# Stick-breaking attention in a hybrid block: two heads' steps taken in turn, on two halves of the PE array

## What is computed

```python
def stick_breaking_attention(q, k, v):
    """A[t,s] = sigmoid(z_ts) prod_{s<j<t} (1 - sigmoid(z_tj)), s < t; q, k, v (B, S, H, d)."""
    ...
        z = jnp.einsum('bqhd,bkhd->bhqk', qb, k).astype(jnp.float32) * scale
        mask = kpos[None, :] < qpos[:, None]
        log_1m = jnp.where(mask, jax.nn.log_sigmoid(-z), 0.0)
        rest = lax.cumsum(log_1m, axis=3, reverse=True) - log_1m
        wts = jnp.where(mask, jnp.exp(jax.nn.log_sigmoid(z) + rest), 0.0)
        return jnp.einsum('bhqk,bkhd->bqhd', wts.astype(v.dtype), v)
```

## Time and profile before

| | us |
|---|---|
| median of the three runs | 3531.89 |
| the three runs | 3523.72, 3532.70, 3531.89 |
| the profiled execution: its time | 3528.36 |
| its span | 3526.5 |

### The profile page before, as it was taken

How to read it: one execution, slowest core, us unless ns; L and a number is a source line. 1 busy time by engine, 2 the same in 40 slices (tenths; PEclk the granted TensorE clock), 3 DMA queues, 4 the chain that set the end, 5 groups by cost and what they waited for, 6 DMA issues and landing times. The chain is left out here.

```text
span 3526.5 us, 59587 instructions
## 1 busy us (share of the span) xinstructions
PE 3337.7 (95%) x24514; PEld 2835.4 (80%) x24514; DVE 2334.9 (66%) x3196; ACT 1581.9 (45%) x2553; POOL 482.5 (14%) x399
## 2 busy tenths in 40 slices
PE   8999999899999899999998999999999989889998
PEld 8998676778998699886767789986899856659986
DVE  7877476448875588754744488755887258658852
ACT  5552435236552455524352365524655253645541
POOL 0003113540003000031125300030000100310001
PEclk9999999999999999999999999999999999999999
DMA  4235211012235223452100122342333222122331
GB/s 157 100 131 186 73 60 38 3 49 96 103 132 160 72 108 108 137 162 73 65 26 4 49 96 103 135 158 73 126 108 106 86 68 72 44 82 85 108 104 64
DMA packets 81589, 327.38 MB, mean 93 GB/s; under 512 B 11904, under 2 KB 11904, under 8 KB 65832
## 3 DMA queue, kind: packets, MB, share of 16 engines
q1 hardware_dynamic: 81320, 323.57, 26.9%
HBM read 321.15 MB, written 4.74 MB: 92 GB/s over the span
## 5 line engine op out<-in xcount | busy, mean ns | idle before, releaser
L235 DVE TENSOR_TENSOR w_low<-w_raw,w_high 128x1024 fp32r<-128x1024 f32 (+1 forms) x241 | 340.2, 1412 | 466.0 <-ACT w_high L227 465.1
L227 ACT ACTIVATE w_high<-w_raw 128x1024 fp32r<-128x1024 f32 (+1 forms) x241 | 284.5, 1182 | 538.0 <-PE ffa_ps L253 172.5
L833 DVE TENSOR_TENSOR w_low<-w_raw,w_high 128x1024 fp32r<-128x1024 f32 (+1 forms) x186 | 220.9, 1187 | 21.4 <-ACT w_high L712 10.7
L712 ACT ACTIVATE w_high<-w_raw 128x1024 fp32r<-128x1024 f32 (+1 forms) x186 | 190.2, 1023 | 3.0 <-PE ffa_ps L253 1.6
L251 PE MATMUL mix_proj_ps<-mix_x_high,w_high 128*128 128x512 f32 x416 | 171.8, 413 | 12.2 <-DVE mix_x_low L400 12.0
L253 PE MATMUL mix_proj_ps<-mix_x_high,w_low 128*128 128x512 f32 x416 | 167.4, 402 | 0.0
L252 PE MATMUL mix_proj_ps<-mix_x_low,w_high 128*128 128x512 f32 x416 | 166.4, 400 | 0.0
L251 PE MATMUL ffa_ps<-ffa_hid_high,w_high 128*128 128x512 f32 x352 | 141.7, 402 | 1.7 <-DVE w_low L235 1.7
L251 PE MATMUL b_f_ps<-b_f_hid_high,w_high 128*128 128x512 f32 x352 | 139.3, 396 | 1.7 <-DVE w_low L235 1.7
L252 PE MATMUL b_f_ps<-b_f_hid_low,w_high 128*128 128x512 f32 x352 | 139.0, 395 | 0.0
L253 PE MATMUL b_f_ps<-b_f_hid_high,w_low 128*128 128x512 f32 x352 | 138.9, 395 | 0.0
(11 more groups left out here) (739 smaller groups left out, 10978.0 us busy)
## 6 DMA issues: line engine op xcount, KB each, us to landing
ffa_quarters<-in_ffa_seven SPq DMA_DIRECT2D x40, 1024.0 KB, 4.8
ffb_quarters<-in_ffb_seven SPq DMA_DIRECT2D x40, 1024.0 KB, 4.8
b_f_quarters<-in_ffn_seven SPq DMA_DIRECT2D x40, 1024.0 KB, 4.9
w_raw<-in_mix_in SPq DMA_DIRECT2D x77, 512.0 KB, 3.4
w_raw<-in_ffa_out SPq DMA_DIRECT2D x32, 704.0 KB, 5.4
w_raw<-in_ffb_out SPq DMA_DIRECT2D x32, 704.0 KB, 5.3
w_raw<-in_ffn_out SPq DMA_DIRECT2D x32, 704.0 KB, 4.1
ffa_ada_raw<-in_w_ada SPq DMA_DIRECT2D x80, 256.0 KB, 2.8
```

The source lines that it names most:

```text
L227: act.activation(self.high[:, self.place(n, 0, kt)], self.raw[:, n % SLOTS, :kt * P], ACT.Copy).then_inc(self.rounded, 1)
L235: dve.tensor_tensor(self.low[:, whole], self.raw[:, n % SLOTS, :kt * P], self.high[:, whole].bitcast(F32), ALU.subtract).then_inc(self.spl ...
L712: act.activation(ops.split(group, r)[0], ops.source(group, r), ACT.Copy).then_inc(part_rounded, 1)
L833: dve.tensor_tensor(low, ops.source(group, r), high.bitcast(F32), ALU.subtract).then_inc(part_split, 1)
```

## The change

The four heads are taken as two pairs, and within a pair the steps alternate: even head, odd head, both with s = 3, then both with s = 2 and so on. Step n belongs to head `n // 8 * 2 + n % 2`.

- The scores of both steps are issued together, in every second slot (`score_pair`), the one on the rows 0 to 63 of the array and the other on the rows 64 to 127, into different banks: four banks are now used by step number and not by s. The wait for a free bank is one step tighter.
- The values of a pair are issued together, alternately for the two heads, the one on the left and the other on the right half of the columns (`values`, with the loop over heads inside). They stand in slots 10 and 19 instead of 6, 10, 14 and 18.
- Between the pairs one slot is left empty: slot 8 issues no scores, slots 9 to 16 belong to the steps 8 to 15. So DVE has no softplus in slot 9, PE no sums in slot 10, and the last sums stand in slot 18 instead of 17. The last values stand behind block 22 instead of block 21.
- `soft` gets a fifth row and `w` one row in another tensor, so that the triangles of two heads find room. The odd head's tiles are stored in the other head's free columns. The buffer of the class `Turner` moves into the tensor of the heads' outputs for that.

No arithmetic is added or taken away: each engine's instructions are the same in kind, size and number, except that some matmuls stand in another order.

```diff
+    PAIR = 2 * NT
     LAG = 2
+    SLOTS = STEPS + 1
+    VALUES = (PAIR + LAG, SLOTS + LAG)
...
+    def at(self, slot):
+        if 0 <= slot < self.PAIR:
+            return slot
+        return slot - 1 if self.PAIR < slot < self.SLOTS else None
+
     def step(self, n):
-        return n // NT, NT - 1 - n % NT
+        return n // self.PAIR * 2 + n % 2, NT - 1 - n % self.PAIR // 2
...
+    def score_pair(self, pe, n):
+        for n in (n, n + 1):
+            hh, s = self.step(n)
+            dims, c = slice(hh % 2 * SBD, (hh % 2 + 1) * SBD), hh // 2
+            at_least(pe, self.w_ready, n - NT + 1)
+            pe.matmul(self.pz[n % NT][:, s * P:], self.m.sk[dims, c, s * P:(s + 1) * P], self.m.sq[dims, c, s * P:],
+                      start=True, stop=True).then_inc(self.z_done, 1)
...
+    def values(self, pe, pair):
+        pe.wait_ge(self.w_masked, self.PAIR * (pair + 1))
+        at_least(pe, self.o_taken, pair)
         for s in range(NT):
-            mm = pe.matmul(self.po[rows, s * P:], self.m.sv[:, s, dims], self.w[:, s, s * P:],
-                           start=s == 0, stop=s == NT - 1, skip_group_check=True)
-        mm.then_inc(self.o_done, 1)
+            for hh in (2 * pair, 2 * pair + 1):
+                dims, rows = slice(hh * SBD, (hh + 1) * SBD), slice(hh % 2 * SBD, (hh % 2 + 1) * SBD)
+                mm = pe.matmul(self.po[rows, s * P:], self.m.sv[:, s, dims], self.weight(hh, s, S - s * P),
+                               start=s == 0, stop=s == NT - 1, skip_group_check=True)
+                if s == NT - 1:
+                    mm.then_inc(self.o_done, 1)
...
-        at_least(dve, self.sum_done, NT * (hh - 1) if s >= NT // 2 else NT * hh)
+        at_least(dve, self.sum_done, n // self.PAIR * self.PAIR)
...
-                    if lag < slot <= sbr.STEPS + lag and (slot - lag) % NT == 0:
-                        sbr.values(pe, (slot - lag) // NT - 1)
-                    if lag <= slot < sbr.STEPS + lag:
-                        sbr.sums(pe, slot - lag)
-                    if 0 <= slot < sbr.STEPS:
-                        sbr.scores(pe, slot)
+                    if slot in sbr.VALUES:
+                        sbr.values(pe, sbr.VALUES.index(slot))
+                    if sbr.at(slot - lag) is not None:
+                        sbr.sums(pe, sbr.at(slot - lag))
+                    if sbr.at(slot) is not None and sbr.at(slot) % 2 == 0:
+                        sbr.score_pair(pe, sbr.at(slot))
```

More of the change, by code:

```diff
@@ L1645, in signals, with place, weight @@
          self.diag_ready, self.sum_done, self.w_ready, self.w_masked, self.o_done, self.o_taken, self.copied_consts) = sems
+    def at(self, slot):
+        if 0 <= slot < self.PAIR:
+            return slot
+        return slot - 1 if self.PAIR < slot < self.SLOTS else None
     def step(self, n):
-        return n // NT, NT - 1 - n % NT
[L1651 to L1662, removed]
+        return n // self.PAIR * 2 + n % 2, NT - 1 - n % self.PAIR // 2
+    def place(self, hh, s, width):
+        if hh % 2 == 0:
+            return s, slice(s * P, s * P + width)
+        return (NT - s if s else NT), slice(0, width)
+    def weight(self, hh, s, width):
+        row, columns = self.place(hh, s, width)
+        return self.w[:, row, columns] if row < NT else self.m.o[:, GC + 1, columns]
+    def score_pair(self, pe, n):
[5 more added lines that the diff above has]
+                      start=True, stop=True).then_inc(self.z_done, 1)
     def sums(self, pe, n):
@@ L1670, in sums @@
         for b in range(NT - 1, s - 1, -1):
+            row, columns = self.place(hh, b, S - b * P)
             for half in range(2):
-                mm = pe.matmul(self.pz[s][:, b * P:], self.sums_of[:, b != s, :],
-                               self.soft[:, half, b, self.columns(hh, b, S - b * P)], start=False, stop=b == s and half == 1,
+                mm = pe.matmul(self.pz[n % NT][:, b * P:], self.sums_of[:, b != s, :],
+                               self.soft[:, half, row, columns], start=False, stop=b == s and half == 1,
                                skip_group_check=True)
         mm.then_inc(self.sum_done, 1)
[L1677 to L1681, removed]
-        for s in range(NT):
-            mm = pe.matmul(self.po[rows, s * P:], self.m.sv[:, s, dims], self.w[:, s, s * P:],
-                           start=s == 0, stop=s == NT - 1, skip_group_check=True)
-        mm.then_inc(self.o_done, 1)
+    def values(self, pe, pair):
+        pe.wait_ge(self.w_masked, self.PAIR * (pair + 1))
+        at_least(pe, self.o_taken, pair)
+        for s in range(NT):
+            for hh in (2 * pair, 2 * pair + 1):
[4 more added lines that the diff above has]
+                    mm.then_inc(self.o_done, 1)
     def softplus_begin(self, dve, n):
@@ L1706, in softplus_end @@
         v = slice(s * P, S)
-        high, low = (self.soft[:, half, s, self.columns(hh, s, S - s * P)] for half in range(2))
+        row, columns = self.place(hh, s, S - s * P)
+        high, low = (self.soft[:, half, row, columns] for half in range(2))
         z, l1 = self.z[:, n % 2, v], self.l1[:, n % 2, v]
         dve.wait_ge(self.log_ready, n + 1)
-        at_least(dve, self.sum_done, NT * (hh - 1) if s >= NT // 2 else NT * hh)
+        at_least(dve, self.sum_done, n // self.PAIR * self.PAIR)
         dve.scalar_tensor_tensor(high, z, 0.0, l1, ALU.max, ALU.add).then_inc(self.high_ready, 1)
@@ L1735, in gpsimd @@
                 hh, s = self.step(n)
-                diagonal = self.soft[:, :, s, self.columns(hh, s, P)]
+                row, columns = self.place(hh, s, P)
+                diagonal = self.soft[:, :, row, columns]
                 pool.wait_ge(self.soft_ready, n + 1)
@@ L1826, in _ @@
                         by_token.take(act, M1_TURNED.index(n - 1), m.sv[:, :, j * P:(j + 1) * P], P)
-                    if lag <= slot < sbr.STEPS + lag:
-                        sbr.weights(act, slot - lag)
-                    if lag < slot <= sbr.STEPS + lag and (slot - lag) % (2 * NT) == 0:
-                        sbr.take(act, (slot - lag) // (2 * NT) - 1)
+                    if sbr.at(slot - lag) is not None:
+                        sbr.weights(act, sbr.at(slot - lag))
+                    if slot in sbr.VALUES:
+                        sbr.take(act, sbr.VALUES.index(slot))
                     if c >= CONVS:
```

38 lines of the change are left out of this document (19 added, 19 removed).

## The result

| | kernel before | changed kernel |
|---|---|---|
| median | 3529.74 us | 3504.65 us |
| spread of the runs | 3523.72 to 3532.7 | 3503.94 to 3511.94 |
| profiled execution, span | 3526.5 | 3502.1 |
| stage of layer 0: first scores to the block behind the last values | 140.3 (18 blocks in it) | 136.57 (19 blocks in it) |
| the same, layer 1 | 143.15 | 136.57 |

The ratio is 0.9937, with a 95% interval of 0.9923 to 0.9951: 22 us less, 17 to 27 (the two medians alone lie 25.1 us apart, with four runs each). The changed kernel was measured again two more times, each time beside the kernel before, with ratios 0.9941 (0.9921 to 0.9961) and 0.9945 (0.9932 to 0.9958). The prediction was 13.6 us less, 3518, with a range down to 3508.

A forecast was written before the change was run, and what follows sets the result against it. PE bounds the stage, DVE close behind over its last blocks. Per layer, 10.2 us saved less 3.4 of waits is 6.8, 13.6 in both: 3531.9 - 13.6 = 3518 us, range 3508 to 3528.

The forecast's parts named there:

- Scores, second head free: PE's paired scores: the second head overlaps on the other row half, costing 0.03 us each.
- Their price: PE's scores, one head: 0.42 to 1.06 us by width, 2.94 together; pairing saves 5.7 us in a layer.
- Values, 4.5: PE's values on alternating column halves: two of four heads hidden, saving 4.5 us in a layer.
- The first wait, 1.4: PE before the first pair's values waits 1.4 us for POOL's mask of step 7's weights.
- E12: End of block 12 on PE; POOL's masks were due 9.0 us after it, PE ready for the values 7.55 after.
- Second and third wait, 2.4 and 2.1: PE before the sums of steps 14 and 15 waits 2.4 and 2.1 us, following DVE's rounds.
- The sum: Per layer, 10.2 us of PE work saved less 3.4 us of added waits: 6.8 us, 13.6 in both.
- Layer 1: Stage of layer 1: shorter by the same about 7 us as layer 0's where the clock is alike.
- Three passes for a pair: Rival on PE's scores: a quarter goes and not half, giving 3523 us; chance 0.06.
- values without overlap: Rival on PE's values: no overlap at 512 columns, 4.5 us less saved in a layer, 3527 us; chance 0.08.
- the slower end: Rival on PE: halves run one after the other and each change of half costs about 0.1 us, 3541 us; chance 0.05.
- The waits do not come: Rival: DVE is earlier than added up, so 5.9 us more is saved in a layer, 3506 us; chance 0.06.

The follow-up runs named there:

- kernels with two: Changed kernel with POOL masking step 7's weights first and the ring's left-out place moved in this stage's run of blocks only: 3507.76 us, ratio 0.9948 to before.
- all three edits: Changed kernel with step 7's mask first, each convolution's first product on ACT, and the ring's left-out place moved in this stage only: 3498.12 us, ratio 0.9923 to before.

## Why the prediction was too cautious, step by step

- **Scores, second head free: right. Their price: wrong, and this is the step that failed.** "One head's scores cost ... 0.42, 0.62, 0.84 and 1.06 us", so 5.7 in a layer. That was read from the scores to the next block. Slot against slot it is 0.62, 0.77, 1.04 and 1.24, 7.3 in a layer: 1.6 more. Half of the visits go, and each costs 0.38 us beyond its columns, of which the distance in the row holds only half.
- **Values, 4.5: right.** Two heads in 2.31 and 2.31 instead of 2.30 each: 4.6.
- **The first wait, 1.4: 0.93,** 0.5 us less. Its cause, the order on POOL, was right: the wait goes with that order. POOL began at E12 + 7.3 (E12 is 463.69 here), as worked out (7.2). But its two masks took 0.73 and 0.46 us and not the 0.91 each of the earlier trace rows, as its timeline in the changed kernel shows:

```profile
470.98 0.73 POOL L1758 TENSOR_TENSOR mix_proj_sb_soft<-mix_proj_sb_soft,squares 128x256 fp32r<-128x256 f32 x1 [8.64 <-DVE mix_proj_sb_soft L1734]
471.67 0.46 POOL L1763 TENSOR_TENSOR heads_out<-heads_out,squares 128x128 f32<-128x128 f32 x1
```

- **Second and third wait, 2.4 and 2.1: 2.46 and 2.00** where the clock doesn't drop. The working from the end of block 18 (16.7 and 25.9 us) held to 0.1. The kernels with two and with all three edits confirm DVE and the rounding as the two bounds.
- **The sum.** PE's work 7.3 + 4.6 = 11.9 less, waits 5.4 instead of 2.5: 9.0 us in a layer by these terms. The stage gives 9.4: 140.3 less 136.57, and 5.65 for the one block more (423.92 to 429.57). The last 0.4 isn't explained; the visits for the values are halved too, from four to two in a layer, and two of 0.2 us outside the row would be 0.4, but this wasn't measured apart.
- **Layer 1.** Before, a drop of the clock behind the last wait cost 2.85 us there (143.15 against 140.3; the earlier trace rows). I kept this cost in the forecast, as if it belonged to the kernel, and counted the clock only as a risk of more. After the scores' price this is the second term that was wrong: its 2.85 us are nearly as much as the scores' miss in both layers, 3.2. In the first profile of the changed kernel the drop falls before step 15's wait, which swallows it. That was luck. In the third profile of the same kernel layer 1's stage is 138.1, with the drop behind the last wait again:

```profile
1748.00:1758.00 10.00, 9.62 (x38) 7.34 (x40) 7.58 (x9) 1.54 (x2) 1.66 (x3) 0.83 0.28 91
```

- **The whole.** 2 x 9.4 + 2.85 = 21.6 of the 24.4 us between the two profiled executions. The other 2.8 lie outside the stages. Three profiles of the changed kernel have spans of 3502.1, 3503.0 and 3505.2 us, so this is no more than they differ by, and I put no cause on it. In the medians a further 2.2 us come from the start of the sum: it was 3531.9, the median of three runs, and the median that the result stands against is 3529.74.
- **Rivals.** Three passes for a pair and values without overlap are out by the rows; so is the slower end, since alternation costs nothing visible (2.31 against 2.30 us). "The waits do not come", at 3506, was next to the measured time by luck: they came, and the gain on PE was larger.

## What to carry to other kernels

Price an operation by comparing two slots that differ in it alone, not by the distance between its row and the next one: what it takes from its neighbours lies outside its row. Half-array matmuls between full-array ones are best gathered: half the visits save PE's time even where nothing overlaps, though the whole is shorter only as far as the other engines follow. And follow a saving on PE to the point where the other engine's chain is anchored: ahead of it all counts, behind it the wait takes it back, and a delay by the clock just before a wait is free as far as the wait reaches.

## What the runs showed of the hardware

- fp32 matmuls of two heads on two row halves of the array overlap in full from 128 to 512 columns, although each is two passes (1.12 us for one head of 512 columns, 1.13 for two). On two column halves they do so when the two heads' matmuls alternate (2.30 us for one head, 2.31 for two); one head after the other, both take 3.86. On the same row half nothing overlaps (384 and 512 columns of one head take 1.77 us).
- One visit of PE from the blocks' matmuls to half-array fp32 scores and back costs 0.38 us beyond the columns, the same in three pairs of slots (12.94 against 13.32, 13.82 against 14.20, 14.42 against 14.81 us). The block's last matmul ahead takes 0.33 instead of 0.23, and the first one behind 0.35, but 0.32 also behind full-array fp32 matmuls.
- A drop of the clock for 3.4 us cost nothing ahead of PE's last wait in the stage (2.00 became 0.48, stage 136.57 against 136.56) and 1.5 us of the stage behind it (138.1).
